# Four gate tiles of a delta rule moved from the scan steps into the delta steps, and three modulation tiles moved to the output projection

## The reference, cut to what matters

```python
mod_l = (silu(c) @ w_ada + b_ada)          # sh1, sc1, g1, sh2, sc2, g2
y = rms_norm(y_ssd * silu(z)) * norm_w_ssd
o = rms_norm(o_gdn) * norm_w_gdn * silu(gate)
x = layer_norm(ALPHA * x + g1 * (concat(y, o) @ w_out))
x = layer_norm(ALPHA * x + g2 * swiglu(x * (1 + sc2) + sh2))
```

## Time and profile before

| | |
|---|---|
| median of 3 runs | 1751.22 us (1748.71 to 1751.86) |
| profiled execution | 1754.71 us, span 1752.9 us |
| PE busy | 1569.8 us (90%) |
| DVE busy | 691.3 us (39%) |
| ACT busy | 375.3 us (21%) |
| POOL busy | 221.1 us (13%) |
| granted clock of PE over the span | 0.956 |
| scan steps, from the first PE product to the rep phase | 1167 to 1264 us |
| delta steps | 1264 to 1442 us |
| output projection and its norm | 1442 to 1515 us |

### The profile page before, as it was taken

The page is one execution under the profiler, slowest core; times in us unless marked ns, Lnnn a source line. Parts: engine busy times, 40 slices in busy tenths (PEclk is TensorE's granted clock), DMA queues, the critical chain, the costliest instruction groups (busy, mean ns, idle before and its releaser), DMA issues.

```text
span 1752.9 us, 22987 instructions
## 1 busy us (share of the span) xinstructions
PE 1569.8 (90%) x9392; PEld 1072.8 (61%) x9392; DVE 691.3 (39%) x1459; ACT 375.3 (21%) x829; POOL 221.1 (13%) x368
## 2 busy tenths in 40 slices
PE   7999999999878787778988889999988889999996
PEld 3548555446555555446666658875667764788842
DVE  2206212424433232534434237777766760400003
ACT  1001255202411111313232213133233320100000
POOL 2000000010000000033124010001255522300000
PEclk9999999998989899889999979999999999999998
DMA  7444343651798989799999943442341143344430
GB/s 253 145 148 162 122 144 111 261 199 73 274 390 326 378 328 400 314 398 390 382 403 379 401 145 132 144 144 96 117 184 49 49 163 139 131 144 146 165 146 24
DMA packets 124285, 372.53 MB, mean 213 GB/s; under 512 B 10523, under 2 KB 26517, under 8 KB 107413
## 3 DMA queue, kind: packets, MB, share of 16 engines
q1 hardware_dynamic: 118245, 361.12, 54.8%
q0 software_dynamic: 1568, 8.39, 1.3%
q10 hardware_dynamic: 4368, 1.54, 0.4%
HBM read 369.98 MB, written 1.05 MB: 212 GB/s over the span
## 4 chain that ended last, share of the span: by engine, by line
PE 71%; DMA 16%; DVE 7%; POOL 2%; ACT 2%; issue 2%; SPq 0%; DVEq 0%; ACTq 0%; POOLq 0%
PE psum L2022 49%; DMA ring<-in_w_up 6%; PE psum L598 6%; DMA ring<-in_w_down 5%; PE psum L1821 4%; DMA ring<-in_w_in 3%; PE psum L2016 2%; PE psum L1862 2%; PE psum L1805 1%; PE psum L1843 1%; POOL area L1614 1%; DVE area L1261 1%; PE psum L623 1%; POOL area L1615 1%; PE psum L2139 1%
## 5 line engine op out<-in xcount | busy, mean ns | idle before, releaser
L2022 PE MATMUL psum<-area,ring 128*128 128x256 f32 (+1 forms) x2048 | 451.0, 380 | 11.7 <-DMA ring<-in_w_in 10.0
L2022 PE MATMUL psum<-ring,area 128*128 128x512 f32 (+1 forms) x1040 | 449.2, 590 | 8.3 <-DMA ring<-in_w_proj_mem 2.1
L2022 PEld LDWEIGHTS psum<-area,ring 128*128 128x128 f32 x2048 | 383.4, 195 | 68.2 <-DMA ring<-in_w_in 14.6
L2022 PEld LDWEIGHTS psum<-ring,area 128*128 128x128 f32 x1040 | 197.0, 191 | 246.6 <-issue 243.0
L598 PE MATMUL psum<-area 128*128 128x128 f32 x1536 | 195.9, 287 | 20.7 <-DVE area L1261 17.5
L598 PEld LDWEIGHTS psum<-area 128*128 128x128 f32 x1536 | 186.4, 200 | 43.4 <-issue 19.8
L1821 PE MATMUL psum<-ring,area 128*32 128x256 f32 x2048 | 137.0, 415 | 57.0 <-DMA ring<-in_w_up 56.9
L2295 ACT ACTIVATE area<-psum 128x512 f32<-128x512 f32 x116 | 66.0, 599 | 454.6 <-PE psum L2022 335.0
L1821 PEld LDWEIGHTS psum<-ring,area 128*32 128x32 f32 x2048 | 70.9, 117 | 108.9 <-issue 80.5
L2016 PE MATMUL psum<-const,area 128*128 128x128 f32 x528 | 84.2, 286 | 21.1 <-DVE area L1349 5.6
L2016 PEld LDWEIGHTS psum<-const,area 128*128 128x128 f32 x528 | 65.2, 146 | 55.0 <-issue 23.9
(11 more groups left out here) (314 smaller groups left out, 1373.0 us busy)
## 6 DMA issues: line engine op xcount, KB each, us to landing
ring<-in_w_gate SPq DMA_DIRECT2D x64, 1024.0 KB, 9.2
ring<-in_w_up SPq DMA_DIRECT2D x64, 1024.0 KB, 10.9
ring<-in_w_down SPq DMA_DIRECT2D x64, 1024.0 KB, 12.1
ring<-in_w_in SPq DMA_DIRECT2D x29, 2048.0 KB, 8.3
...
```

Source lines behind the costliest of these rows:

```text
L2022: last = nc.tensor.matmul(dst, lhs(k), rhs(k), start=first and k == 0, stop=final and k == count - 1)
```

## The change

The scan steps held all eight gate tiles, two in each. They now hold z's four (`GATES`), one in each step, in step 7 between gram 4 and rep 4. The delta gate's four tiles gt leave the scan steps and stand behind the delta phases kS 4, v 4, v 5 and v 6 (`GATE_PHASES`), on PE and on ACT. The modulation tiles come in the order 8, 9, 4, 5, 6, 7, 10, 11 (`MODS`); none stands behind v 4, v 5 and v 6 any more. The first two stand at cross 4 and expand 4, four at u 7, w 7, v 7 and out 7, and the last two, with three sums, between the pieces of the output projection (`between_w2`). The stream of weights is put in the same order. POOL loads the rows of the modulation's bias in two DMAs (`mod_rows[:, 0:2]`, g1 and sh2, only behind out 6, since they lie where the gate tiles' input lies), and its multiply by the gain moves from u 5 and u 6 to out 5 and out 6. `modulate` waits for the second DMA from its third tile on. POOL's wait for all modulation tiles now ends in the output projection.

```diff
-    after = ["xb0", "xb1", "xb2", "k0", "k1", "v0", "v1", "q0", "q1", "gt0", "gt1", "z0", "z1"]
-    after += [f"ad{i}" for i in range(4, 12)] + [f"w2{i}" for i in range(4)]
+    after = ["xb0", "xb1", "xb2", "k0", "k1", "v0", "v1", "q0", "q1", "z0", "z1"]
+    after += ["ad8", "ad9", "gt0", "gt1", "ad4", "ad5", "ad6", "ad7", "w20", "ad10", "w21", "ad11", "w22", "w23"]
...
-        MOD_PHASES = ["cross 4", "expand 4", "kS 4", "v 4", "v 5", "v 6", "u 7", "w 7", "v 7"]
-        GATES = [(kind, i, t) for kind in ("gt", "z") for i in range(2) for t in range(NT)]
+        MODS = (8, 9, 4, 5, 6, 7, 10, 11)
+        MOD_PHASES = {"cross 4": (None, 0), "expand 4": (0, 1), "kS 4": (1, None), "u 7": (None, 2), "w 7": (2, 3), "v 7": (3, 4), "out 7": (4, 5)}
+        GATE_PHASES = {"kS 4": (0, 0), "v 4": (0, 1), "v 5": (1, 0), "v 6": (1, 1)}
+        GATES = [("z", i, t) for i in range(2) for t in range(NT)]
...
                 if i < 3:
-                    gate_tiles(GATES[2 * i:2 * i + 1])
+                    gate_tiles(GATES[i:i + 1])
...
                 if i == 3:
                     assert next(delta_steps) == "rows 4"
-                    gate_tiles(GATES[6:7])
                     assert next(delta_steps) == "gram 4"
-                    gate_tiles(GATES[7:8])
+                    gate_tiles(GATES[3:4])
                     assert next(delta_steps) == "rep 4"
-                else:
-                    gate_tiles(GATES[2 * i + 1:2 * i + 2])
...
+                if next_tile is not None:
+                    mod_part(next_tile)
+                if phase in GATE_PHASES:
+                    gate_tiles([("gt",) + GATE_PHASES[phase]])
...
+            def between_w2(n):
+
+                if n:
+                    mod_sum(4 + n)
+                if n in (1, 2):
+                    mod_part(5 + n)
+                if n == 2:
+                    turn_o()
...
             root(o_root[:, 0, :])
+            for n in (6, 7):
+                part_out(n)
...
             normed_o(0)
+            for n in (5, 6, 7):
+                modulate(n)
...
-                if phase in ("u 5", "u 6"):
+                if phase == "out 6":
+                    wait_filled(eng, ("gt", 1, 1))
+                    eng.dma_start(mod_rows[:, 0:2, :].rearrange("p i d -> p (i d)"), a["b_ada_2"][0, 2 * D:4 * D].partition_broadcast(P))\
+                       .then_inc(s["rows2_in"], 16)
+                if phase in ("out 5", "out 6"):
```

77 lines of the change are left out of this document (38 added, 39 removed).

## The result

| | before | after |
|---|---|---|
| median of the runs, us | 1751.54 (4 runs, 1748.71 to 1758.0) | 1780.31 (4 runs, 1775.76 to 1782.72) |
| ratio after : before | | 1.0149, 95% interval 1.0119 to 1.018 |
| profiled execution, us | 1754.71 | 1775.76 |
| its span, us; mean granted clock | 1752.9; 0.956 | 1774.0; 0.946 |

The changed kernel is 28.8 us slower by the medians. The forecast was 1771 with a range of 1759 to 1777: the sign was right, and the time lies 3.3 us above the range.

What follows compares the result with a forecast made beforehand. PE's chain was taken to bound scan and projection, with DVE close behind, and PE and DVE alternating in the delta steps. Terms summed to +20.5 us, some 1771 on the median of 1751.2; range of 8 in 10: 1759 to 1777.

Steps and rivals of the forecast that it cites:

- scan steps, up to rep 4's start (-3.5 and -0.8): Scan: gate tiles gone save 8.9, three pauses cost 5.4, net -3.5; rep 4 starts 0.8 earlier.
- step 5 (to M 5): Behind v 4: a gate tile of 6.87 replaces 0.86 + 1.85 ahead of cross and out, nothing hides it: +4.15.
- step 6 (M 5 to M 6): Gate tile behind v 5 +4.15; POOL's multiply leaves u 5, -1.3, and returns at out 5, +0.65: together +3.5.
- step 7 (M 6 to M 7): Gate tile behind v 6, 2.95 after DVE's old wait, plus 0.95 for POOL's multiply and DMA issue: +3.9.
- tail (M 7 to w20): Modulation sums and parts around u 7, v 7 and out 7 delay the projection's start: +2.8 - 0.86 = +1.9.
- output projection (w20 to w23): Three sums and two parts between pieces, all on PE's chain, with weights arriving in time: +6.3.
- POOL's multiplication at the norm: POOL's late preparation holds DVE's L1525 from W + 9.6 to W + 14.9, W the projection's last piece's start: +5.3.
- So a long pause costs 1.6 to 1.8, taken as 1.8. Three pauses: 5.4.: PE's idle time ahead of y_inner in three scan steps lowers the clock; cost read from rep and M: 5.4.
- (a): Rival at the norm: no collision between DVE and POOL; +15.7, 1767 us. Chance 0.17.
- (b): Rival in the scan: clock holds, pauses of 3.6 and rep 4 cost nothing; 1764.5 us. Chance 0.13.
- (c): Rival: gate tiles fill PE's pauses, M 5 to M 7, rep 6 and t 6 at full clock; 1750. Chance 0.06 faster, 0.07 level.
- (d): Rival in the projection: the ring of weights is one unit late, a wait of up to 8; 1779 us. Chance 0.07.

Runs made afterwards that it cites:

- e1: Changed kernel with six (step 4) or four filling matmuls, never read, in the pauses ahead of y_inner in scan steps 4 to 6: 1764.94 us, ratio 1.0098 to before.
- e4: Changed kernel with only POOL's second multiply by the gain moved, from out 6 to u 7: 1777.36 us, ratio 1.0174 to before.
- h2: Changed kernel with as many filling matmuls as e1, but weights of 32 columns instead of 128: 1772.95 us, one run.
- e3: Changed kernel with POOL holding its multiplication by ALPHA until both halves of the norm are done: 1776.77 us, ratio 1.0171 to before.
- j1: Kernel before with only the last modulation products moved between the output projection's units, gates left in the scan: 1751.56 us, ratio 1.0012 to before.
- e2: Changed kernel with gate tiles behind kS 5 to 7 instead of v 4 to 6, gain multiplies at u 6 and u 7: 1767.32 us, ratio 1.0117 to before.
- f2: Changed kernel with e2's and e3's edits, modulation tiles 8 to 10 in the scan's pauses, none in the projection: 1747.86 us, ratio 1.0002 to before.
- i1: Changed kernel's tiles reordered: two gate tiles at scan step 4, gt partly at kS 4 to 6, modulation tiles at kS 7, e3's wait: 1747.86 us, ratio 0.9993 to before.
- f1: Changed kernel with the edits of e1, e2 and e3 together: 1747.36 us, ratio 0.9986 to before.
- h1: Changed kernel with three, two and one filling matmuls of 512 columns ahead of y_inner in scan steps 4, 5 and 6: 1763.24 us, one run.
- k1: i1 with filling matmuls in remaining pauses, tile 11's part at kS 4, its sum taken by DVE behind out 6: 1736.50 us, ratio 0.9929 to before.

## Why the prediction was wrong in size

By its own steps, in microseconds against before; the measured numbers are differences between the traces of after and before, start to start, rounded each.

| step of the forecast | forecast | measured |
|---|---|---|
| scan steps, up to rep 4's start (-3.5 and -0.8) | -4.3 | +3.5 |
| rep 4 at the low clock, up to M 4 | +1.6 | +1.1 |
| M 4 without its pause | -1.8 | -1.7 |
| step 5 (to M 5) | +4.15 | +3.8 |
| step 6 (M 5 to M 6) | +3.5 | +2.5 |
| step 7 (M 6 to M 7) | +3.9 | +5.4 |
| tail (M 7 to w20) | +1.9 | +4.3 |
| output projection (w20 to w23) | +6.3 | +6.6 |
| POOL's multiplication at the norm | +5.3 | +5.3 |
| sum | +20.5 | +30.7 |

**The step that failed is "So a long pause costs 1.6 to 1.8, taken as 1.8. Three pauses: 5.4."** The rest of that working stands. From step 5's gate tile to its y_inner it took 15.45 us before and takes 12.22 now: 3.23 less, where 3.25 had been worked out. But from y_inner to the next gate tile it takes 12.31 at step 4 and 11.99 at step 5 instead of 7.48, and from y_inner of step 6 to the next y_state 10.09 instead of 5.76: 4.8, 4.5 and 4.3 us for the three pauses, 13.6 instead of 5.4. The 1.8 had been read from M, where the clock came back after some 3.6 us of matmuls. In y_inner it did not come back in 7 us, and the state's products behind it were slow too. e1 shows that it is the clock: rep 4 stands 11.8 us earlier with the three pauses filled. In the forecast this term had one value, though the earlier trace rows bounded it for other matmuls only; a bound from above (y_inner wholly at half speed, 3.5 more, and L580 behind it 1.4 more) would have given 3 x 4.9 = 14.7 instead of 5.4, and a range up to 1786 that holds the result.

The clock's fall itself was foreseen. The Trainium skill's "TensorE: Matmul & The Clock Gate", section "HAM oscillation — how this bites in real kernels", has each burst of matmuls start at the low clock again in a loop whose bursts are shorter than its waits. At y_inner the trace agrees in all three steps, at a granted clock of 0.50, though the bursts here are longer than the waits; at M 6, behind 3.04, it does not, at 1.00.

**Step 7 was mis-sized by 1.5.** The forecast said: "L1671 (2.36) and a DMA issue stand in POOL's program right there, 0 to +2.4, taken 0.95." The rows show that DVE's addition was held across POOL's multiplication and the two instructions behind it, 5.05 us in all instead of 0.68 (the earlier trace rows had 1.2 of waiting in this place, and DVE's L1261 took 3.90 there instead of 2.39). From the end of cross to the end of expand DVE needs 9.3 us instead of 7.9. One operation was held by three of POOL's in a row, so the length of one was no upper bound. e4 gave back 2.2 of it at M 7. Two changes of the clock that the forecast did not have cancel within this row: M 6 takes 3.84 instead of 5.47, and rep 7 4.09 instead of 2.42. That they do is luck.

**The tail was mis-sized by 2.4.** M 7 and the product behind it take 8.39 instead of 7.25: 1.1. The pause ahead of them grew from 5.22 to 6.61, but that this is the cause is not shown: in h2 they take 7.04 behind the same 6.61. ACT's table load stands in front of the copy that t 7 needs: 0.72. Before there is none at u 7. The gate tile behind v 6 brings it, since its Silu has ACT load another table at 1394.29, between two uses of the root's. That leaves 0.6 of the 2.4, which no row names. The forecast said of ACT's copies "neither is late"; one was.

**What was right.** M 4, steps 5 and 6, the projection and the norm came within 1 us of their terms, the last two within 0.3. The pair of TENSOR_SCALARs of DVE and POOL, which no row of before had shown, excluded each other for the whole length: 5.48 for a 0.75, as the forecast took from the neighbouring row. The Trainium skill's "SBUF — State Buffer", section "Who interferes with whom", has it so too, and the trace agrees: L1540 ends 0.55 behind the end of L1707. e3 and j1 show it from both sides: held back, the 4.7 us are gone; with the modulation tiles moved alone, they are there. That the term fits to 0.1 is in part luck. By the forecast's own rows POOL would end at W + 8 + 5.36 = W + 13.4 and the term be some 4.6; it was rounded up to W + 14, and POOL's multiplication took 5.68 instead of 5.36. The forecast's sum without this meeting is +15.2, too, not the +15.7 of rival (a); 0.5 us, which changes nothing.

**The rivals.** (a), no meeting at the norm: refuted by L1540. (b), the clock holds: refuted by the windows at 0.50. (c), the tiles fill the pauses: refuted at M 5, M 6 and M 7, which wait 3.03, 3.04 and 6.61, though M 6 and t 6 did run at full clock as it had them; e2 shows that the tiles fill the pauses of M 5 and M 6 when put behind kS, and leave 3.78 of M 7's. (d), a late unit in the projection: refuted, TensorE waits for no weights there.

**What stays open.** Why 32 records of 64 columns don't bring the clock back when 32 of 128 columns do was not tested apart. Nor is it settled what decides for pauses between 1.9 and 3.2 us. At rep 6 the same pause of 2.12 to 2.13 held the clock in e2, f2, h2 and i1 (2.42 to 2.43) and lost it in after, e1, e3, e4, f1, h1 and k1 (3.27 to 4.12). M 5 behind 3.03 or 3.04 took 3.84 in h1 and 5.36 to 5.47 in after, e1, e3, e4 and h2. 1.91 (i1, behind a modulation part) fell, and in f2 the clock fell within y_inner 0.77 us behind such a part and held one step later. Every pause of 1.52 held, and at y_inner and M the clock had fallen behind every one from 3.18 on. Something besides the length decides; no run here isolates it. That the narrow weights of a modulation part are it is made unlikely by h2.
